# The first gated MLP's first product as seven half-size products with its convolution by halves, and both MLPs in a new order

## The reference, cut to what matters

```
# first block: a causal depthwise convolution of width 3 along the tokens between the products
h  = rmsnorm(x, ffn_norm_g)
up = causal_depthwise_conv(h @ w_up, conv_w, conv_b)     # 1024 x 5632
a, bgate = split(up, 2)
x  = x + (silu(a) * bgate) @ w_down
# third block
gate, up = split(h @ w_gate_up, 2)                       # 1024 x 5632
ffn = (silu(gate) * up) @ w_down
h   = layer_norm(ALPHA * h + ffn)
```

## Time and profile before

| | us |
|---|---|
| median of 3 runs | 3181.14 (3180.71 to 3182.11) |
| the profiled execution, its time | 3180.48 |
| its span in the profile | 3179.2 |
| PE busy | 3003.6 (94% of the span) |
| DVE busy | 1780.6 (56%) |
| ACT busy | 1150.5 (36%) |

### The profile page before, as it was taken

One profiled execution on the slowest core, in us unless ns is written; L12 is line 12 of the kernel. 1 busy time (PEld: TensorE's weight loads), 2 busy tenths in 40 slices (PEclk: granted clock), 3 DMA queues, 4 the chain that ended last, 5 costly groups with the idle time before them and its releaser, 6 DMA issues.

```text
span 3179.2 us, 34027 instructions
## 1 busy us (share of the span) xinstructions
PE 3003.6 (94%) x13986; PEld 2355.1 (74%) x13986; DVE 1780.6 (56%) x2535; ACT 1150.5 (36%) x1708; POOL 2.2 (0%) x6
## 2 busy tenths in 40 slices
PE   7999798999999997999998989999988899999997
PEld 5887687888888875877775757665556688888885
DVE  4442336444454447676774453667663866666666
ACT  3223413222222225344445434555642522222223
POOL 0000000000000000000000000000000000000000
PEclk9999999999999998999999999999989999999999
DMA  3211011111111111111110111000001111111111
GB/s 136 79 59 44 30 47 40 47 47 48 52 49 51 44 49 34 40 40 33 34 33 20 33 33 34 28 21 27 21 20 40 34 47 53 60 47 54 58 49 66
DMA packets 48823, 141.61 MB, mean 45 GB/s; under 512 B 12790, under 2 KB 16670, under 8 KB 48542
## 3 DMA queue, kind: packets, MB, share of 16 engines
q1 hardware_dynamic: 48670, 139.45, 14.0%
HBM read 135.16 MB, written 9.77 MB: 46 GB/s over the span
## 4 chain that ended last, share of the span: by engine, by line
PE 85%; ACT 6%; DVE 5%; issue 3%; DMA 0%; SPq 0%; ACTq 0%; DVEq 0%
PE psum L508 37%; PE psum L744 13%; PE psum L974 10%; PE psum L784 8%; PE psum L542 5%; PE psum L564 2%; PE psum L553 2%; PE psum L901 1%; PE psum L884 1%; PE psum L1056 1%; PE psum L1083 1%; PE psum L559 1%; DVE residual L1940 1%; ACT sb_left L1769 1%; DVE swa_p L2539 0%
## 5 line engine op out<-in xcount | busy, mean ns | idle before, releaser
L508 PE MATMUL psum<-h_hi,w_hi 128*128 128x512 f32 x1408 | 438.6, 393 | 6.6 <-ACT ret_q L1261 2.9
L508 PE MATMUL psum<-h_hi,w_lo 128*128 128x512 f32 x1408 | 434.0, 389 | 0.0
L508 PE MATMUL psum<-h_lo,w_hi 128*128 128x512 f32 x1408 | 434.0, 389 | 0.0
L1925 DVE TENSOR_TENSOR w_lo<-w_raw,w_hi 128x1024 fp32r<-128x1024 f32 x164 | 200.4, 1222 | 255.9 <-ACT w_hi L1168 255.5
L508 PEld LDWEIGHTS psum<-h_hi,w_hi 128*128 128x128 f32 x1408 | 262.8, 188 | 65.8 <-issue 13.0
L508 PEld LDWEIGHTS psum<-h_lo,w_hi 128*128 128x128 f32 x1408 | 264.3, 188 | 55.3
L508 PEld LDWEIGHTS psum<-h_hi,w_lo 128*128 128x128 f32 x1408 | 264.3, 188 | 55.2
L2166 DVE TENSOR_TENSOR residual<-residual,psum 128x1024 f32<-128x1024 f32 x176 | 214.5, 1219 | 141.6 <-PE psum L784 70.3
L1168 ACT ACTIVATE w_hi<-w_raw 128x1024 fp32r<-128x1024 f32 x164 | 172.5, 1052 | 227.3 <-PE psum L508 181.7
L974 PE MATMUL psum<-h_hi,w_hi 128*128 128x512 f32 x576 | 211.6, 447 | 5.2 <-ACT y L1180 2.3
L974 PE MATMUL psum<-h_hi,w_lo 128*128 128x512 f32 x576 | 204.1, 414 | 0.0
(11 more groups left out here) (332 smaller groups left out, 5256.4 us busy)
## 6 DMA issues: line engine op xcount, KB each, us to landing
w_raw<-in_weights SPq DMA_DIRECT2D x228, 512.0 KB, 3.5
residual<-in_x_t SPq DMA_DIRECT2D x8, 512.0 KB, 9.2
out_t<-residual SPq DMA_DIRECT2D x8, 512.0 KB, 3.0
rel_copies<-rel_rows SPq DMA_DIRECT2D x8, 480.0 KB, 6.2
na_bias<-rel_copies SPq DMA_DIRECT2D x8, 240.0 KB, 4.1
band_copies<-band_rows SPq DMA_DIRECT2D x8, 192.0 KB, 6.2
ret_rotary<-in_rotary SPq DMA_DIRECT2D x1, 1024.0 KB, 7.5
swa_bias<-band_copies SPq DMA_DIRECT2D x4, 256.0 KB, 2.8
```

Of the source, the lines that this page charges most:

```text
L508: ins = self.pe.matmul(out[:, s], w[:, k, at:at + P], src(k, low)[:, s], start=(k == 0 and part == 0), stop=(k == n_k - 1 and part == 2))
L1925: self.dve.tensor_tensor(self.m.w_lo[:, n % 2, :], self.m.raw[:, n % 2, :], self.m.w_hi[:, n % 2, :].bitcast(F32), ALU.subtract).then_inc( ...
```

## The change

Both MLPs take one program, mlp(plan, norm), with a Plan each. In both, column tiles 0 and 1 are plain (96 matmuls each) and tiles 2 to 21 take the seven products. For the first MLP this puts 84 matmuls where 96 were, 20 times; for the last one tile 1 goes back from 84 to 96. The four sums of the first MLP's input come out of eight buffers mlp_normed that split_norm now fills.

The order of the seven blocks becomes G1, S2, S1, G2, S4, S3, U2, on the banks (0, 1, 3, 0, 3, 2, 2), so that the first half of the gate's tokens (c11, bank 0) is whole after the fourth block and its second half (c12, bank 3) after the fifth. The weight sums need one buffer instead of two. In the last MLP the product silu(gate)*up becomes one instruction of 1024 tokens (gated_product) instead of two of 512.

The convolution of the gate is done by halves: 512 tokens from bank 0 (taps_a), two tokens carried over (dve_carry), 512 from SBUF (taps_a2). That of the up part is done on 1024 tokens from SBUF (mlp_cb), after the tile's last block: tap_b on ScalarE, and linear on VectorE, which stands at the head of the step after that block. The core of the diff:

```
-    G1, S2, S3, S1, G2, U2, S4 = range(7)
+    G1, S2, S1, G2, S4, S3, U2 = range(7)
...
-        self.stages = [("up", 1)]
+        self.stages = []
...
-        bank = (0, 1, 2, 3, 0, 2, 3)
-        emptied = (("act_c11" + name, c), ("dve_u2" + name, c), ("dve_c21" + name, c), ("dve_c12" + name, c))
-        read = {4: ("act_s1" + name, c), 5: ("dve_u3" + name, c), 6: ("dve_c22" + name, c)}
+        bank = (0, 1, 3, 0, 3, 2, 2)
+        c11_read = ("dve_carry", c) if plan is PLAN1 else ("act_c11" + name, c)
+        emptied = {0: c11_read, 1: ("dve_u2" + name, c), 2: ("dve_c12" + name, c), 5: ("dve_c21" + name, c)}
+        read = {3: ("act_s1" + name, c), 4: ("dve_u4" + name, c), 6: ("dve_c22" + name, c)}
...
     def products(self, plan, c, j):
...
         elif j == 5:
+            self.after("dve_u4" + name, c)
+            dve.tensor_tensor(m.vs, m.vs, bank[2], ALU.add).then_inc(*to("dve_c22" + name, c))
         elif j == 6:
+            self.after("dve_c12" + name, c)
+            dve.tensor_tensor(m.us, m.us, bank[2], ALU.add).then_inc(*to("dve_c21" + name, c))
...
+    def linear(self, c):
+
+        m, channel = self.m, c + DFF // P
+        self.tap("b", 1, m.tp[:, 1:S], m.cb[:, 0:S - 1], channel, (c, 1), ("act_tap_b", c))
+        self.tap("b", 2, m.tp[:, 2:S], m.cb[:, 0:S - 2], channel, (c, 2), ("dve_tap_b", c, 1))
+        self.gated_tile(c)
...
     def mlp1(self):       # VectorProgram
...
+        for n in range(1, len(plan.blocks) + 1):
+            ahead = 4 <= n + 2 < len(plan.blocks)
+            kind, c, j = plan.blocks[n - 1]
+            done = plan.last_up(n - 1)
+            if done is not None:
+                self.linear(done)
+                if done == 2 * NGROUP - 1:
+                    self.hidden("mlp1", done)
+            if ahead:
+                self.block_sums(plan, n + 2)
+            if kind == "up":
+                self.products(plan, c, j)
             else:
...
+                for o in (2 * j, 2 * j + 1):
+                    half = (c - plan.base) % 2
+                    self.add_down(c, half, o)
...
+            if ahead:
+                self.block_low(plan, n + 2)
+            if kind == "up":
+                self.conv_step(plan, c, j)
...
+    def conv_step(self, plan, c, j):
+        if c == 2:
+            if j == 0:
+                for k in range(4):
+                    self.input_low(plan, k, 3)
+            elif j == 1:
+                self.hidden("mlp1", 0)
+            elif j == 2:
+                self.plain_taps("a", plan.a[1], self.m.ta, 1, 1)
+            elif j == 3:
+                self.plain_taps("b", plan.b[1], self.m.tp, 1, 1 + DFF // P)
+                self.gated_tile(1)
+            elif j == 4:
+                self.hidden("mlp1", 1)
+                self.taps_a(c)
+        elif j == 0 and c % 2 == 0:
+            self.hidden("mlp1", c - 1)
+        elif j == 3:
+            self.taps_a(c)
+        if j == 5:
+            self.taps_a2(c)
```

More of the change, by code:

```diff
@@ L301, in raw_free @@
         for n, (kind, i, j) in enumerate(self.blocks):
[L302 removed]
+            if (kind, j) == ("up", self.S4) and self.a[i] == t or (kind, j) == ("up", self.U2) and self.b[i] == t:
                 return "mw_lo_" + self.name, n
@@ L671, in mean_after_mix, with mlp @@
         self.column_mean("mean1024", self.m.n_acc, ("pe_n2_mean",), ("act_n2_rstd", 1))
[L673 to L703, removed]
+    def mlp(self, plan, norm):
         m, q, on, name = self.m, self.q, self.on, plan.name
+        read = ((lambda c: ("dve_tap_a", c, 2), lambda c: ("dve_tap_b", c, 2)) if plan is PLAN1 else
+                (lambda c: ("act_gate" + name, c), lambda c: ("dve_m" + name, c)))
         self.n_acc += self.n_acc % 2
-        self.project_pair(lambda k: (f"act_{norm}_hi", k), lambda k: (f"dve_{norm}_lo", k), ("act_gate" + name, 0), ("dve_m" + name, 0))
+        self.project_pair(lambda k: (f"act_{norm}_hi", k), lambda k: (f"dve_{norm}_lo", k), read[0](0), read[1](0))
+        for i in range(2):
+            t = self.tile
+            q.wait_ge(*on("w_lo", t))
+            out = self.take(("proj", t), 4 + 2 * i, 2, read[i](1))
+            self.gemm(out, KD, *self.weights(t), 0, self.h).then_inc(*self.to("proj", t))
+            self.tile += 1
         for kind, i in plan.stages:
@@ L743, in seven @@
                 for part, (w, x) in enumerate(((w_hi, high), (w_lo, high), (w_hi, low))):
-                    ins = self.pe.matmul(out[bank[j]], w[:, k, :], x(k), start=(j < 4 and k == 0 and part == 0),
+                    ins = self.pe.matmul(out[bank[j]], w[:, k, :], x(k), start=(j in emptied and k == 0 and part == 0),
                                          stop=(k == 3 and part == 2), skip_group_check=True)
@@ new lines, in product @@
+        def product(c):
+            q.wait_ge(*on("act_gatemlp3", c))
+            q.wait_ge(*on("proj", plan.b[c]))
+            if c:
+                self.after("dve_hid_lomlp3", c - 1)
+            else:
+                self.after("dve_t_lomlp3", 3, 2)
+            dve.tensor_tensor(m.tp[:], m.ta[:], m.place["proj", plan.b[c]], ALU.mult).then_inc(*to("dve_mmlp3", c))
+        sums(0)
+        self.split_up_to(plan.base + 2)
+        self.input_low(plan, 0, 1, 0, 2)
+        sums(1)
+        self.split_up_to(plan.base + 3)
@@ L2633, in mlp3 @@
+        self.input_low(plan, 1, 1, 0, 2)
+        for k in range(2, 4):
+            sums(k)
+            self.input_low(plan, k, 1, 0, 2)
         self.block_sums(plan, 1)
@@ L2659, in mlp3 @@
                 self.products(plan, c, j)
-                if j == 6 and c == 2 * NGROUP - 1:
-                    self.hidden("mlp3", c)
+                if j == 6:
+                    self.gated_product(plan, c)
+                    if c == 2 * NGROUP - 1:
+                        self.hidden("mlp3", c)
             else:
-                half = plan.blocks[n - 1][1] % 2
+                half = (c - plan.base) % 2
                 last = c >= plan.d[2 * NGROUP - 2]
@@ L2671, in mlp3 @@
                 self.block_low(plan, n + 2)
-            if kind == "up" and j == 0 and c > 1 and c % 2 == 0:
+            if (kind, c, j) == ("up", 2, 0):
+                for k in range(4):
+                    self.input_low(plan, k, 3)
+            elif (kind, c, j) == ("up", 2, 1):
+                product(1)
+            elif (kind, c, j) == ("up", 2, 2):
+                self.hidden("mlp3", 1)
+            elif kind == "up" and j == 0 and c % 2 == 0:
                 self.hidden("mlp3", c - 1)
@@ L2713, in block_sums @@
         g, u = m.raw[:, plan.a[i] % 2, :], m.raw[:, plan.b[i] % 2, :]
-        before = plan.first["up", i - 1] if i > 1 else None
         if j == plan.S2:
```

530 lines of the change are left out of this document (300 added, 230 removed).

## The result

| kernel | median us | runs, lowest to highest | ratio to before, 95% interval |
|---|---|---|---|
| before | 3180.71 | 6, 3178.98 to 3182.11 | |
| after | 3192.73 | 6, 3187.61 to 3194.72 | 1.0034 [1.0022, 1.0046] |
| after, timed again later | 3188.57 | 6, 3187.51 to 3194.35 | 1.0032 [1.0021, 1.0044] |

What follows compares the result with a forecast made beforehand. TensorE, busy for 94% of the span, was taken as the bound. Matmuls and pauses saved, 71 us, against 75 us of new short waits summed to +3.4 us, about 3185 us on the median; range 3169 to 3205.

Steps and rivals of the forecast that it cites:

- matmuls: Both MLPs: the first loses 20 x 12 matmuls, -54.4 us; the last gains 12, +2.7 us.
- pause at the first MLP's start: First MLP, after the first pair of tiles: TensorE's wait for a bank goes, -1.2 us.
- start of the last MLP: Plain tile 1 covers VectorE's input sums, so TensorE's pause and its lower clock go, -12.7 us.
- end of the first MLP: Matmuls needing only tile 20 cover 5.4 us of the wait before the last down outputs; -5.8 us.
- c22, 40: Each seven-product tile: TensorE waits 1.11 us between sixth and seventh block for VectorE's read of their shared bank; +44.5 us.
- linear before the third down output, 10: After ten even tiles the first add stands behind linear, so TensorE waits 1.96 us each; +19.6 us.
- u4 in even tiles, 9: First MLP, even tiles after an odd one: VectorE's u4 comes 0.34 us late for TensorE; +3.1 us, bounds 0 and 9.
- tile 2 of the first MLP: First seven-product tile: VectorE's long queue delays c22, a pause of 6.9 us with lower clock after it; +7.6 us.
- Rival A: Bank handover at VectorE's pace of 0.61 us with the restart hidden, 12.6 us off the sum: 3172 us; chance 0.2.
- Rival B: VectorE becomes the bound of the first MLP: +28 us, so 3213 us, or 3199 at half of that; chance 0.25.
- idle time before the fifth block: Sign against the forecast: TensorE idle there in even tiles would mean VectorE is the bound.
- Rival C: The clock falls in the short pauses too: 40 x 1.85 = +74 us, 3259 us; chance 0.04.

Runs made afterwards that it cites:

- e2: Kernel after, with the first two down-output adds placed between and behind linear's taps on VectorE instead of after linear; 3170.28 us, 0.9971 of before.
- e6: Kernel after, with S3's block before S4's in the last MLP only, plus the changes of e2 and e3; 3139.05 us, 0.9866 of before.
- e0: Kernel after, unchanged and timed again; 3188.57 us, 1.0032 of before.
- e3: Kernel after, with the odd tile's hidden split made after the even tile's third block in the first MLP; 3185.06 us, 1.0015 of before.
- e7: Kernel after, with S3's block before S4's in the first MLP only and ScalarE's tap_b ahead of its silu; 3192.13 us, 1.0039 of before.
- e8: e7 with VectorE's c21 ahead of taps_a2; 3178.07 us, 0.9988 of before.
- e1: Kernel after, with S3's block before S4's in both MLPs, the two reading each other's weights; 3183.68 us, 1.0014 of before.
- e4: e1 with each block reading its own weights; 3183.34 us, 1.0010 of before.
- e5: Kernel after, with S3's block before S4's in both MLPs, tap_b ahead of silu, and the changes of e2 and e3; 3115.80 us, 0.9800 of before.
- e9: e5 with VectorE's c21 ahead of taps_a2; 3113.42 us, 0.9787 of before.

## Why the prediction was right in its mechanism and 8 us short

Its terms beside what the trace of after shows, in us:

| term | predicted | measured | from |
|---|---|---|---|
| matmuls | -54.4 + 2.7 | the same | 228 fewer |
| pause at the first MLP's start | -1.2 | -1.2 | no pause |
| start of the last MLP | -12.7 | -12.9 | pause of 10.44 and 40.52 - 38.08 before, neither in the chain of after |
| end of the first MLP | -5.8 | -5.7 | last add starts 30.5 after the up tiles, was 36.2 |
| c22, 40 | +44.5 | +42.0 | 40 x (0.94 + 0.11) |
| linear before the third down output, 10 | +19.6 | +20.3 | 1.88 + 0.12, one of 2.25 |
| u4 in even tiles, 9 | +3.1 | +7.2 | 9 x (0.69 + 0.11) |
| tile 2 of the first MLP | +7.6 | +7.3 | 5.77 + 2.57 of slow matmuls - 1.05 of c22 |
| sum | +3.4 | +5.3 | |

The stages' own times agree. The final mean's sums start 8.0 us later than before (3151.58 against 3143.56 us); of that the terms give 5.3, and 2.7 lie in small differences of the stages around them (1.1 in the first MLP, 1.1 between the MLPs, 0.5 in the last). The rest of the span's 11.3 us, 3.3, comes behind the last MLP, in code that the change doesn't touch:

```profile
3151.58 3.07 PE L788 MATMUL psum<-norm_acc,common 128*128 128x512 f32 x4 [2.45 <-DVE norm_acc L2727]
3154.45 2.53 PE L788 MATMUL psum<-residual,common 128*128 128x512 f32 x4
```

In the trace of before each such four took under 2 us (1.99 and 1.88). The windows view gives the granted clock of 3151 to 3158 us as 0.76 here (1.00 in the same stage of before):

```profile
3151.00:3158.00 7.00, 5.40 (x8) 2.03 (x8) 1.51 (x2) 0.00 (x0) 0.00 (x0) 0.76 0.00 0
```

The other traces show part of why. The chain behind the last MLP, first in e2, then in e6:

```profile
3130.16 5.41 PE psum L788 x8
...
3137.96 14.67 PE psum L561 x30
```

```profile
3102.29 3.71 PE psum L794 x8
...
3108.39 13.16 PE psum L565 x30
```

The eight matmuls take 5.41 us, and the thirty behind them 14.67 to 14.73, in all six traces whose last MLP has the c22 stops (after, e0, e2, e3, e7, e8), and 3.71 or 3.72 and 13.16 in all six without them (before, e1, e4, e5, e6, e9). TensorE's stop just ahead of the eight is the same in both groups, 2.61 us. So these 3.3 us go with the stops in the last MLP and are a cost of the change that my sum had at nothing; how stops that end 27 us earlier bring it about, no run shows.

Of the 7.9 us between the sum's 3.4 and the span's 11.3, these 3.3 and the 2.7 around the stages were in no term. The terms themselves are off by 1.9 together, which is partly luck: c22 came out 2.5 lower, u4 4.1 higher. **The term that was mis-sized is u4 in even tiles**: 0.34 us each, measured 0.80. VectorE's timeline behind an odd tile, whose last block ends at 605.57:

```profile
605.77 0.69 DVE L2837 TENSOR_TENSOR mlp_cb<-mlp_cb,psum 128x512 f32<-128x512 f32 x1 [0.40 <-PE psum L731]
...
608.21 2.60 DVE L2177 SCALAR_TENSOR_TENSOR mlp_tp<-mlp_cb,vectors,mlp_tp 128x1023 f32<-128x1023 f32 x2 [1.15 <-ACT mlp_tp L1306]
...
613.27 1.23 DVE L2297 TENSOR_TENSOR mlp_act_lo<-mlp_tp,mlp_act_hi 128x1024 fp32r<-128x1024 f32 x1 [0.53 <-ACT mlp_act_hi L1944]
...
616.40 0.68 DVE L2827 TENSOR_TENSOR mlp_cb<-mlp_cb,psum 128x512 f32<-128x512 f32 x1
```

linear starts 2.64 us behind the block, where I had 2.10. ScalarE's tap is what is late: ahead of it ScalarE has a weight split that waits for S1's sum, and a silu:

```profile
605.46 0.63 ACT L1934 ACTIVATE w_hi<-w_raw 128x512 fp32r<-128x512 f32 x1 [2.87 <-DVE w_raw L2868]
606.00 1.04 ACT L1327 ACTIVATE mlp_ta<-mlp_ta 128x1024 f32<-128x1024 f32 x1
606.95 1.23 ACT L1306 ACTIVATE mlp_tp<-mlp_cb,vectors 128x1024 f32<-128x1024 f32 x1
```

I had followed VectorE's queue through this stretch and had taken ScalarE as free at c21's end. So u4 ends at 617.08, 11.5 us behind the block instead of 11.0. The bounds that I gave for this term (0 to 9) hold it.

The other steps stand. c22 pauses in every seven-product tile, at 1.05 us instead of 1.11. In the prediction's text on it one count is wrong: in the old order two blocks, not three, lay between the two that share c22's bank; nothing hangs on it. The Trainium skill's rule, weight loads pulled ahead of matmuls in flight ("TensorE: Matmul & The Clock Gate", Part 2), does not help behind these waits: the weight load of the c22 stop starts with its matmul at 602.71, and 0.11 us of restart is lost at each stop. Rival A (a cheaper handover) is refuted, the handover takes the full 0.69. Rival B (VectorE as the bound) is right in one small place, u4, and wrong as a bound of the MLP, which e5 shows. I had named idle time before the fifth block as a sign that VectorE is the bound, though my own sum had 0.34 us there in nine tiles; as a sign it was badly chosen. Rival C, the clock falling in short pauses, is wrong for the 38 stops of 0.7 to 2.25 us in the first MLP's groups, apart from the 3.3 us behind the last MLP, but e7 and e8 show where it begins to be right. The rule of the Trainium skill in Part 1 of the same page, small gaps that bring the lower clock back again and again, fits the stops of e7 (3.2 to 3.5 us), and not those 38.

So the change saves 71 us and gives them back in 59 short stops. None of them lies in the seven products as such: each is a place in an order. With the seven products kept and five places in the queues moved (e9: the swap, the adds, the hidden, tap_b, taps_a2), the kernel is 68 us faster than before.

## What to carry to other kernels

When a change orders accumulations anew, write down for each bank which read lies between the two blocks that use it: back to back, the handover cost 1.05 us each time here, with VectorE busy for only 61% of the span. After taking one wait away, look at who stands behind it in the in-order queues (e1 and e7 lost the whole gain of the first MLP that way), and try the removals together, since the adds inside linear are worth 18 us alone and also make the swap worth its 21 in the first MLP (e5 against e6, with tap_b first: 23). Follow every queue of a chain in such a sum, ScalarE's too, not only that of the engine that seems to be late.

## What the runs showed of the hardware that I had not expected

Most short stops left the granted clock alone and slightly longer ones did not. In the first MLP's groups of the kernel after, all 38 stops of 0.69 to 2.25 us (the first tile's apart) were followed by matmuls at 2.4 GHz. After all ten of e7's stops before a third down output, 3.2 to 3.5 us, about eight matmuls ran at 1.2 GHz. Of e8's ten the first, 4.06 us, was too; of its nine of 2.53 to 2.67 us six were followed by such matmuls and three were not, though they stand at the same place of like groups; compare these two of e8, 2.53 us each:

```profile
628.85 0.73 PE L777 MATMUL psum<-mlp_act_hi,w_hi 128*128 128x512 f32 x2 [2.37 <-DVE residual L2297]
...
629.93 1.05 PE L777 MATMUL psum<-mlp_act_lo,w_hi 128*128 128x512 f32 x2
630.79 1.05 PE L777 MATMUL psum<-mlp_act_hi,w_hi 128*128 128x512 f32 x2
```

```profile
692.96 0.73 PE L777 MATMUL psum<-mlp_act_hi,w_hi 128*128 128x512 f32 x2 [2.37 <-DVE residual L2297]
...
694.00 0.62 PE L777 MATMUL psum<-mlp_act_lo,w_hi 128*128 128x512 f32 x2
```

The length alone does not decide it: near the end of the first MLP a stop of 3.09 us in the kernel after and one of 3.45 in e7 were followed by matmuls at full speed. And the one c22 stop that is left in tile 2 under the swap, 2.13 to 2.16 us in e1, e4, e5, e7, e8 and e9, was followed by slow matmuls in e4, e7 and e9 and by none in e1, e5 and e8. In e9 eight of them come a few matmuls behind it, 0.43 us apart:

```profile
552.83 0.50 PE L737 MATMUL psum<-h_hi,w_hi 128*128 128x512 f32 x1 [2.00 <-DVE mlp_cb L2845]
...
554.33 0.63 PE L737 MATMUL psum<-h_lo,w_hi 128*128 128x512 f32 x1
554.76 0.63 PE L737 MATMUL psum<-h_hi,w_hi 128*128 128x512 f32 x1
```

So in the first MLP 2.1 us is the shortest stop that a fall followed, inside the 0.7 to 2.25 us of the kernel after. A fall makes the loss behind a stop 1.75 us where it is 0.12 to 0.15 otherwise, so where the stop grew from 1.9 us (after) to 3.3 (e7) the loss grew by 1.4 + 1.6. Of the 12 us between the profiled executions of e7 and e8, 6.4 are stop (7.0 less in nine together, 0.7 more in the first) and 4.8 are three falls fewer there.
